# Memory cross attention cut into halves of the tokens and set between the mixer's output product, its norms and its own output product

## The reference, cut to what matters

```python
x = layer_norm(ALPHA * x + merged @ w_out, ln1_g, ln1_b)            # end of the hybrid mixer

q = (x @ w_q).reshape(Bsz, S, X_HEADS, HEAD_DIM) * (HEAD_DIM ** -0.5)   # 4 heads of 64
k, v = jnp.split(mem @ w_kv, 2, axis=-1)
p = jax.nn.softmax(jnp.einsum('bshd,bmhd->bhsm', q, k).astype(jnp.float32), axis=-1)
o = jnp.einsum('bhsm,bmhd->bshd', p, v).reshape(Bsz, S, X_HEADS * HEAD_DIM)
x = layer_norm(ALPHA * x + o @ w_o, ln2_g, ln2_b)

a, b = jnp.split(x @ w_in, 2, axis=-1)                              # feed-forward, D_FF = 2816
x = layer_norm(ALPHA * x + (jax.nn.silu(a) * b) @ w_out, ln3_g, ln3_b)
```

## Time and profile before

| | us |
|---|---|
| median of 3 runs | 907.75 (906.89 to 908.51) |
| profiled execution | 908.46, of which the span of the core is 906.7 |
| TensorE busy | 886.0 (98%) |
| VectorE busy | 423.8 (47%) |
| ScalarE busy | 290.6 (32%) |
| GpSimd busy | 59.0 (7%) |
| mean granted clock of TensorE | 0.993 |

### The profile page before, as it was taken

The page is one execution under the profiler, slowest core; times in us unless marked ns, Lnnn a source line. Parts: engine busy times, 40 slices in busy tenths (PEclk is TensorE's granted clock), DMA queues, the critical chain, the costliest instruction groups (busy, mean ns, idle before and its releaser), DMA issues.

```text
span 906.7 us, 11683 instructions
## 1 busy us (share of the span) xinstructions
PE 886.0 (98%) x4579; PEld 736.6 (81%) x4579; DVE 423.8 (47%) x795; ACT 290.6 (32%) x536; POOL 59.0 (7%) x87
## 2 busy tenths in 40 slices
PE   9999999999999999999999889999999999999996
PEld 9988897777578888888889679888888888888885
DVE  3344346669632525344757684333433333422344
ACT  3112157129632222222414642222222222111221
POOL 2100000081310000000020020000000000000001
PEclk9999999999999999999999899999999999999998
DMA  7524521420003332326605101233322224223321
GB/s 268 158 93 132 124 94 26 135 80 19 2 7 104 104 111 93 93 93 232 208 25 185 47 2 53 93 107 107 103 93 93 93 93 139 93 95 98 109 95 70
DMA packets 70023, 89.89 MB, mean 99 GB/s; under 512 B 2701, under 2 KB 61911, under 8 KB 69983
## 3 DMA queue, kind: packets, MB, share of 16 engines
q1 hardware_dynamic: 69599, 88.92, 30.1%
q0 software_dynamic: 384, 0.43, 0.3%
HBM read 86.81 MB, written 2.52 MB: 99 GB/s over the span
## 4 chain that ended last, share of the span: by engine, by line
PE 92%; ACT 3%; DVE 3%; issue 1%; POOL 1%; DVEq 0%; POOLq 0%; ACTq 0%
PE ps L1590 27%; PE ps L1592 27%; PE ps L1591 27%; PE ps L1798 3%; PE ps L1762 3%; PE ps L1727 2%; ACT prob L851 2%; PE ps L1627 1%; DVE w_lo L1083 1%; PE ps L2070 1%; PE ps L1649 1%; PE ps L2071 1%; PE ps L2072 1%; DVE xt_lo L1089 0%; ACT w_hi L829 0%
## 5 line engine op out<-in xcount | busy, mean ns | idle before, releaser
L1590 PE MATMUL ps<-xt_hi,w_hi 128*128 128x512 f32 (+1 forms) x712 | 274.5, 386 | 5.6 <-DVE w_lo L1083 2.6
L1591 PE MATMUL ps<-xt_hi,w_lo 128*128 128x512 f32 (+1 forms) x712 | 273.7, 384 | 0.0
L1592 PE MATMUL ps<-xt_lo,w_hi 128*128 128x512 f32 (+1 forms) x712 | 273.6, 384 | 0.0
L1590 PEld LDWEIGHTS ps<-xt_hi,w_hi 128*128 128x128 f32 x712 | 133.8, 188 | 33.7 <-DVE w_lo L1083 3.5
L1592 PEld LDWEIGHTS ps<-xt_lo,w_hi 128*128 128x128 f32 x712 | 133.8, 188 | 26.7
L1591 PEld LDWEIGHTS ps<-xt_hi,w_lo 128*128 128x128 f32 x712 | 133.8, 188 | 26.2
L829 ACT CAST w_hi<-raw 128x1024 fp32r<-128x1024 f32 (+1 forms) x59 | 60.8, 1035 | 184.5 <-PE ps L1592 172.7
L1083 DVE TENSOR_TENSOR w_lo<-raw,w_hi 128x1024 fp32r<-128x1024 f32 (+1 forms) x59 | 71.3, 1212 | 97.5 <-ACT w_hi L829 97.2
L1546 DVE TENSOR_TENSOR w_lo<-raw,w_hi 128x1024 fp32r<-128x1024 f32 x40 | 48.9, 1222 | 79.1 <-ACT w_hi L1042 79.1
L1367 DVE TENSOR_TENSOR w_lo<-raw,w_hi 128x1024 fp32r<-128x1024 f32 x30 | 36.7, 1223 | 91.5 <-ACT w_hi L968 91.5
L1042 ACT CAST w_hi<-raw 128x1024 fp32r<-128x1024 f32 x40 | 41.9, 1047 | 78.8 <-PE ps L1592 78.8
(11 more groups left out here) (256 smaller groups left out, 1282.2 us busy)
## 6 DMA issues: line engine op xcount, KB each, us to landing
raw<-in_w_in SPq DMA_DIRECT2D x24, 1024.0 KB, 5.0
raw<-in_w_ffn_in SPq DMA_DIRECT2D x22, 1024.0 KB, 4.9
raw<-in_w_ffn_out SPq DMA_DIRECT2D x11, 1024.0 KB, 4.9
raw<-in_w_mix_out SPq DMA_DIRECT2D x4, 1024.0 KB, 4.9
x_nat<-in_x SPq DMA_DIRECT2D x4, 512.0 KB, 5.6
raw<-in_w_branch_b SPq DMA_DIRECT2D x4, 512.0 KB, 3.9
resid<-in_x SPq DMA_DIRECT2D x1, 2048.0 KB, 9.8
raw<-in_w_xkv SPq DMA_DIRECT2D x2, 1024.0 KB, 5.2
```

The costliest lines, as they stand in the source:

```text
L1590: pe.matmul(dst, a_hi, b_hi, start=start, stop=False)
L1591: pe.matmul(dst, a_lo, b_hi, start=False, stop=False)
L1592: return pe.matmul(dst, a_hi, b_lo, start=False, stop=stop)
```

## The change

The pieces change places: the memory's keys and values come first, ahead of the mixer's output product. Of tile 3 of that product, the first half of its columns is made as before, then the queries of tiles 0 and 1 (256 tokens), two of the six products of the second half of the columns, the scores of the first half, and the other four. The queries of the second half are made for tile 2 and tile 3 apart, with 128 columns each. The probabilities are no longer scaled ahead of their transposes. The inverted sums are spread over 64 columns a head by GpSimd (`widen_cross`), transposed by TensorE (`turn_recip_cross`, 4 transposes a half), copied by ScalarE to `xr`, and VectorE multiplies the product with the values by them (`cross_out`, for two heads at once). High and low part are then cut from `xm` in SBUF, for two heads at once. The drain of the first half lies ahead of the output product of tile 0, that of the second half ahead of tile 2's. The scores of the second half, and the transposes of its probabilities, use PSUM banks 4 to 7. `slot_spent` and the tiles in SBUF are laid out anew to fit this.

```diff
-PM = 63
-PKX = 71
-PVX = 73
+PKX = 63
+PVX = 65
+PM = 67
...
+            def widen_cross(half_t):
+                c = stat_col("X", 0, 2 * half_t)
+                pool.wait_ge(rsum_ready, N_OUT - N_AH + half_t + 1)
+                if half_t:
+                    pool.wait_ge(recip_ps, N_OUT - N_AH + 1)
+                for i in range(2):
+                    pair = rsum[:, c + 4 * i:c + 4 * i + 4].rearrange("p (h t) -> p t h", t=2)
+                    pool.tensor_copy(xw[:, i, :, :].rearrange("p t (h d) -> p t h d", h=2),
+                                     pair.unsqueeze(3).to_broadcast([P, 2, 2, DH])).then_inc(recip_wide, 1)
...
+            def cross_turned(half_t):
+                for h in range(N_XH):
+                    pt_drain(gx + N_XH * half_t + h)
+                act.wait_ge(recip_ps, N_OUT - N_AH + half_t + 1)
+                if half_t:
+                    act.wait_ge(xm_done, 2)
+                act.copy(xr[:, :, :].rearrange("p i c -> p (i c)"), ps[:, X_RECIP, :]).then_inc(recip_out, 1)
+            def cross_hi(k):
+                act.wait_ge(xm_done, k + 1)
+                q0 = 256 * (k // 2)
+                act.copy(ox_hi[:, k % 2, q0:q0 + 256], xm[:, k % 2, :]).then_inc(ox_hi_done, 1)
...
             square(0)
             square(1)
             turn_tile(1, 0)
             square(2)
             turn_tile(1, 1)
-            square(3)
-            turn_tile(1, 2)
-            for p in range(PVX, PXO + 2):
-                split(p)
-            turn_tile(1, 3)
             for h in range(N_XH):
                 exps(N_SELF, h)
+            turn_tile(1, 2)
+            square(3)
+            cross_turned(0)
+            split(PXO)
+            cross_hi(0)
+            split(PXO + 1)
+            cross_hi(1)
+            turn_tile(1, 3)
...
             split(PF)
-            gx = groups_before[N_SELF]
+            split(PF + 1)
+            square(TT)
             for h in range(N_XH):
                 exps(N_SELF + 1, h)
-                if h == 0:
-                    split(PF + 1)
-                if h >= 1:
-                    pt_drain(gx + h - 1)
-            for n in range(gx, groups_before[N_JOB] + 1, 2):
-                for m in xaccs_ended[n - 2] if n > gx else []:
-                    cross_hi(m)
-                for nn in (n + 2, n + 3):
-                    if gx + 3 <= nn < groups_before[N_JOB]:
-                        pt_drain(nn)
-            square(TT)
             square(TT + 1)
...
+            cross_turned(1)
+            split(PF + 2)
+            cross_hi(2)
+            split(PF + 3)
+            cross_hi(3)
...
+            def cross_out(k):
+                if k % 2 == 0:
+                    dve.wait_ge(recip_out, N_OUT - N_AH + k // 2 + 1)
+                dve.wait_ge(av_done, acc_end[FIRST_X + 2 * k + 1] + 1)
+                if k >= 2:
+                    dve.wait_ge(oxl_done, k - 1)
+                dve.tensor_tensor(xm[:, k % 2, :], ps[:, acc_bank(FIRST_X + 2 * k), 0:256], xr[:, k % 2, :], ALU.mult).then_inc(xm_done, 1)
+            def cross_lo(k):
+                dve.wait_ge(ox_hi_done, k + 1)
+                q0 = 256 * (k // 2)
+                dve.tensor_tensor(ox_lo[:, k % 2, q0:q0 + 256], xm[:, k % 2, :], f32(ox_hi[:, k % 2, q0:q0 + 256]),
                                   ALU.subtract).then_inc(oxl_done, 1)
...
+            memory_key_out(0)
+            rest_of(PVX)
+            memory_key_out(1)
+            rest_of(PVX + 1)
+            rest_of(PM)
...
+            norm_sums(3, (0,))
+            queries_out(0, 256, 0, 0)
...
+            norm_sums(3, (1,))
+            cross_sums(0)
+            turn_tile(1, 2)
+            norm_out(3)
+            queries_out(256, P, 6, 2)
+            cross_out(0)
+            rest_of(PXO)
+            cross_out(1)
+            cross_lo(0)
+            rest_of(PXO + 1)
+            cross_lo(1)
+            turn_tile(1, 3)
...
+            queries_out(384, P, 6, 4, PXQ)
+            norm_out(TT)
...
+            cross_sums(1)
+            turn_tile(2, 0)
             norm_out(TT + 1)
-            turn_tile(2, 0)
+            cross_out(2)
+            rest_of(PF + 2)
+            cross_out(3)
+            cross_lo(2)
+            rest_of(PF + 3)
+            cross_lo(3)
+            turn_tile(2, 1)
...
+            pe.wait_ge(mem_lo, 4)
+            pe.wait_ge(sig_done, N_PAIR * 6)
+            for n in range(2):
+                pe.wait_ge(lo_done, PKX + n + 1)
+                tile_piece(PKX + n, 4 + n, memt_hi, memt_lo, slice(0, MEM))
+            pe.wait_ge(merged_even, N_PAIR)
+            for n in range(2):
+                pe.wait_ge(lo_done, PVX + n + 1)
+                v_piece_two(pe, PVX + n, w_hi, w_lo, memt_hi, memt_lo, ps, 4 * n, range(2), lambda t: (6, 256 * t), mm3, natural).then_inc(piece_done, 1)
             pe.wait_ge(merge_step, 12)
...
-            rows_tail(PM, KT, N_TAIL, 3, m_hi, m_lo)
-            turn_tile(1, 2)
...
+            rows_tail(PM, KT, N_TAIL, 3, m_hi, m_lo, halves=(0,))
...
+            gx = groups_before[N_SELF]
+            pe.wait_ge(turn_lo, 2 * TT + 4)
+            queries(0, 256, 0)
+            rows_tail(PM, KT, N_TAIL, 3, m_hi, m_lo, halves=(1,), part=slice(0, 2))
+            pe.wait_ge(xq_out, 2)
+            scores(N_SELF)
+            rows_tail(PM, KT, N_TAIL, 3, m_hi, m_lo, halves=(1,), part=slice(2, None))
+            turn_tile(1, 2)
+            cross(0)
             pe.wait_ge(turn_lo, 2 * TT + 6)
-            queries(0)
+            turn_recip_cross(0)
+            pe.wait_ge(y_done, 2 * TT)
+            queries(256, P, 6)
+            times_v(gx)
+            pe.wait_ge(recip_out, N_OUT - N_AH + 1)
+            times_v(gx + 2)
+            pe.wait_ge(xq_out, 4)
             turn_tile(1, 3)
-            pe.wait_ge(xq_out, 2)
-            pe.wait_ge(memkv_out, 3)
-            scores(N_SELF)
+            pe.wait_ge(oxl_done, 2)
+            rows_tail(PXO, 2, 2, 0, ox_hi, ox_lo)
             pe.wait_ge(turn_lo, 2 * TT + 8)
-            queries(1)
-            pe.wait_ge(xq_out, 4)
+            queries(384, P, 6, last=True)
+            rows_tail(PXO, 2, 2, 1, ox_hi, ox_lo, halves=(0,))
+            pe.wait_ge(xm_done, 2)
+            pe.wait_ge(xq_out, 6)
             scores(N_SELF + 1)
-            gx, g_end = groups_before[N_SELF], groups_before[N_JOB]
-            turn_probs(gx)
-            turn_probs(gx + 1)
-            for n in range(gx, g_end, 2):
-                if n + 2 < g_end:
-                    turn_probs(n + 2)
-                    turn_probs(n + 3)
-                times_v(n)
-                if n == gx + 4:
-                    pe.wait_ge(oxl_done, N_XH)
-                    pe.wait_ge(neg_ready, units_before[N_JOB])
-                    rows_tail(PXO, 2, 2, 0, ox_hi, ox_lo)
-            rows_tail(PXO, 2, 2, 1, ox_hi, ox_lo)
-            pe.wait_ge(oxl_done, 2 * N_XH)
+            rows_tail(PXO, 2, 2, 1, ox_hi, ox_lo, halves=(1,))
+            turn_tile(2, 0)
+            cross(1)
+            pe.wait_ge(pt_act, pt_count(gx + N_XH + 1)[1])
+            turn_recip_cross(1)
+            times_v(gx + N_XH)
+            pe.wait_ge(recip_out, N_OUT - N_AH + 2)
+            times_v(gx + N_XH + 2)
+            turn_tile(2, 1)
```

More of the change, by code:

```diff
@@ L485, in scale_units @@
                     f = factor[:, t, 0, h:h + 1]
-                elif kind in ("A1", "A2"):
+                else:
                     f = factor_s[:, 0 if kind == "A1" else 1, t, h:h + 1]
-                else:
-                    n = stat_col(kind, h, t)
-                    f = rsum[:, n:n + 1]
                 yield prob_at(kind, at, cols), f
         def scaled_before(j):
-            scaled = [k for k in range(N_JOB) if k < N_AH or k >= N_SELF]
-            return sum(len(JOBS[k][2]) for k in scaled if k <= j and (k in POOL_SCALES) == (j in POOL_SCALES))
+            return sum(len(JOBS[k][2]) for k in range(j + 1) if (k in POOL_SCALES) == (j in POOL_SCALES))
         def scaled_for(j, g):
-            read = (3, 8, 8, 12)[g] if j < N_AH else 2 * (g + 1)
-            after = len(JOBS[j][2]) - read
+            after = len(JOBS[j][2]) - (3, 8, 8, 12)[g]
             return scaled_before(j) - after
@@ L528, in split_slot @@
         def split_slot(p):
-            for first, n, hi, lo in ((PM + 2, 4, x_hi, x_lo), (PKX, 2, k_hi, k_lo), (PXQ, 3, c_hi, c_lo), (PXO + 1, 1, k_hi, k_lo)):
+            for first, n, hi, lo in ((PM + 2, 4, x_hi, x_lo), (PXQ, 2, k_hi, k_lo), (PXO, 2, c_hi, c_lo)):
                 if first <= p < first + n:
@@ L973, in _ @@
             gate_iteration(N_PAIR - 1, True)
-            for p in range(PM + 1, PM + 8):
+            for p in range(PKX + 1, PXQ):
                 split(p)
             act.wait_ge(merge_step, 2 * N_PAIR * 6)
-            split(PKX)
-            split(PKX + 1)
+            split(PXQ)
+            split(PXQ + 1)
             def square(n):
@@ L1416, in norm_sums @@
                     dve.wait_ge(resid_in, 16)
-                for c in range(2):
```

(37 more changed lines are left out.)

205 lines of the change are left out of this document (82 added, 123 removed).

## The result

| | before | after |
|---|---|---|
| median | 907.03 us (6 runs, 906.75 to 908.51) | 913.88 us (6 runs, 913.43 to 914.53) |
| profiled execution | 908.46, span 906.7 | 914.03, span 912.3 |
| mean granted clock of the profiled execution | 0.993 | 0.996 |

The account below looks back on a forecast made before the run. TensorE's list plus its waits bounds the kernel. Products +5.2, transposes +0.9, waits +3.5, old clock fall -3.5, new fall +1.0 make +7.1 us on 907.75: 914.9 us, range 909.6 to 926.

Parts of the forecast that it names:

- Work added: TensorE's list: second-half queries as 96 products at 0.115 us, +5.2 us; 8 more transposes for the inverses, +0.9.
- Rivals 1 and 2: 128-column query products: cheap at 0.070 us, 910.6 us, chance 0.2; dear at 0.227 us, 925.7 us, chance 0.15.
- rival 3: Whole kernel: no change, with cheap query products and the clock staying up, 909.6 us; chance 0.07.
- `w_lo` of the first values piece: Ahead of the values: TensorE waits 1.5 us, to 437.75, while VectorE copies keys and makes the rest.
- first drain: First half's output, near 510 us: TensorE waits 2.2 us for VectorE's 3.7 us chain with two weights rests.
- copy to `ptx`: Second half's inverses, near 529 us: TensorE waits 2.7 us for ScalarE's copy behind exponentials, a square and two casts.
- second drain: Second half's output, near 535 us: TensorE waits 2.8 us for `oxl_done` behind a norm and VectorE's 3.7 us chain.
- The mixer's first weights: Mixer's first two pieces: load and rests stay hidden by 0.1 to 0.4 us; each us of delay would be lost.
- I expect the fall near 529: Second half's inverses and values products: slow clock stretches them about 2.6 us, mostly swallowed by the next wait; +1.0 us.
- The credit for the slow clock of before: Stretch 506.04 to 519.30 us of the kernel before: its slow clock cost 3.5 us, which the change removes.
- 6.8 us together: Same stretch of the kernel before: 32 transposes and three products with the values at full clock take 6.8 us.
- Rival 4: Both drains and the `ptx` copy: their waits don't come, so the kernel is faster, 904.7 us with none left; chance 0.08.

Follow-up runs that it names:

- q_narrow: The changed kernel with the first half's queries also cut into 128-column pieces, 96 products instead of 48; 917.21 us, ratio 1.0107.
- values_early: The changed kernel with VectorE making the first value piece's rests ahead of the last gate merge's last two steps; 910.95 us, ratio 1.0043.
- first_drain: The changed kernel with the two output pieces' rests made ahead of the first half's output instead of between its steps; 910.80 us, ratio 1.0035.
- q_wide: The changed kernel with the second half's queries made once, 48 products of 256 columns instead of twice 48 of 128; 912.70 us, ratio 1.0058.
- warm_before: The kernel before with 8 identity products filling TensorE's 2.25 us wait for probabilities; 907.47 us, ratio 0.9996.
- orders_warm_wide: orders_warm with second-half queries made once at 256 columns, copied earlier by VectorE, and identity products ahead of the first half's output product; 908.94 us, ratio 1.0022.
- warm_all: The changed kernel with 7, 8 and 8 identity products in its three waits behind 508 us; 912.19 us, ratio 1.0054.
- orders_warm: The changed kernel with value, output and first-layer rests reordered, plus 8 identity products ahead of the second half's inverses; 908.03 us, ratio 1.0009.

## Why the prediction was right, point by point

**Direction and size.** Forecast +7.1 and 914.9 us; measured +6.85 and 913.88. Of the 1.0 us by which 914.9 is too high, 0.7 lie in its base: 907.75 was the median of three runs, 907.03 is that of six. The direction rests on its mechanism, dearer products and new waits, and both were seen. That the size fits so well is in part luck: the sum in the profiled executions is smaller, +5.6, and its terms show where errors cancelled.

**Work added.** Forecast 96 products at 0.115 us, +5.2; the trace has 0.114 and 0.117, 11.1 us for 5.85, and q_narrow repeats the price (5.0 us for 48 more). Rivals 1 and 2 are out, and rival 3 with the first. The figure of the Trainium skill (TensorE: Matmul & The Clock Gate, section Back-to-back issue gap), about 81 ns for a pair with 128 columns, gives by estimate 7.8 us for the 96; this float32r pair takes 0.114, and the measurement decides. The reason that I gave, that each product loads a new tile of weights, agrees with it, since halving the columns saved only 7%; that the load is what binds is argued and was not measured apart. A slower pace per column at 128 columns would space the products alike, and the trace records each weights load with 0.19 us, whether 128, 256 or 512 columns follow.

**Waits.** Forecast 10.2 us in place of 6.7; the trace has 8.5, so +1.8 instead of +3.5.

| | forecast | trace |
|---|---|---|
| `w_lo` of the first values piece | 1.5 | 1.5 |
| `xt_lo` of tile 2 | 0.3 | none |
| first drain | 2.2 | 2.0 |
| exponentials | 0.7 | 0.2 |
| copy to `ptx` | 2.7 | 2.4 |
| second drain | 2.8 | 2.4 |

Each large one stands where it was put, with its releaser, and the two drains and the values' rest went away when their order was changed (the second drain's without a gain in time, since the norm and a fall took its place). The mixer's first weights came in time, as forecast. VectorE made their rests at (timeline of the changed kernel):

```profile
441.96 1.22 DVE L1099 TENSOR_TENSOR w_lo<-raw,w_hi 128x1024 fp32r<-128x1024 f32 x1 [2.96 <-ACT w_hi L842]
...
444.85 1.23 DVE L1099 TENSOR_TENSOR w_lo<-raw,w_hi 128x1024 fp32r<-128x1024 f32 x1 [0.45 <-ACT w_hi L842]
```

**The clock.** This step was wrong in place, in size and in its use. "I expect the fall near 529": it came behind the first drain, at about 512, and cost 1.4 us on the twelve products behind that wait, not 1.0. In values_early, first_drain and q_wide it came between 526 and 530 after all, and there the second drain's wait swallowed a part of it, as forecast: it was 1.7, 1.0 and 1.2 us instead of 2.4. The credit for the slow clock of before was too large: "6.8 us together" at full clock is 7.3 in warm_before, which makes the credit 2.9 and not 3.5. With the forecast's 3.5 the terms give 5.2 + 0.9 + 1.8 - 3.5 + 1.4 = 5.8, by which the stage did grow (the two spans differ by 5.6); with 2.9 they give 6.4, and 0.6 us of it stay unexplained. And the credit belongs to the profiled execution. The median execution of before loses less to its clock: its runs at 0.997 are 1.8 us faster than those at 0.993, and its median is 1.4 us under the profiled execution, where that of the changed kernel is 0.15 under. That turns 5.6 into 6.85. The forecast added +7.1, worked out against one execution, to a median; its waits were 1.7 us too long, its credit for a median execution was too large by about as much, and that the two errors cancelled is luck.

**Rival 4**, that the waits don't come, is out: they came. That memory keys ahead of the mix cost or give anything beyond the 1.5 us wait was not tried by itself; with that wait gone, the stage up to the queries shows no other.

**What the change is worth.** Its loss has three parts of different kinds: 5.2 us of products, of which q_wide gets back only some 2 in the trace (1.2 between medians), and orders_warm_wide nothing; some 4 us of order, which three reorderings won back; and 1.5 us of clock by warm_all (the stage of orders_warm, with both repaired, is 5.6 us shorter). They add up to more than 6.85 because the change also removed the waits and the slow stretch of before. With the last two repaired the divided form comes within 0.1% of the undivided one (ratio 1.0009) and does not beat it.

## What to carry to other kernels

Cutting float32r products from 256 to 128 columns cost here almost the whole price per product; count such a split as doubled work on TensorE's list before counting what it overlaps. In a two-step drain between engines (cast on one, rest on the other), look for weights work placed between the steps: moving 2.3 us of it ahead took the wait from 2.0 to 0.4 us, but moving it behind delayed the next norm by 1.2. Compare executions by their mean granted clock before crediting a stretch of slow clock to a kernel: the profiled one may be an unusual one.
